# A decoder block's mixer: products of the chunk kernel over four column groups, the first convolution tap on ScalarE, low parts of weights split at other places

## What is computed

```
x = x + 1/2 * SwiGLU(RMSNorm(x))
h = RMSNorm(x); [u | v | gates] = h @ w_in          # 1024 -> 5120
y_a = GLU(GELU(S5(u)))          # 64 groups of 16 channels, 64 complex states each, + d_skip * u
y_b = ConformerConv(v)          # z = val * sigmoid(gate); causal depthwise conv of 31 taps; LayerNorm, SiLU, pointwise
x = x + (sigmoid(g_A) * y_a + sigmoid(g_B) * y_b) @ w_out
x = x + 1/2 * SwiGLU(RMSNorm(x)); final RMSNorm
```

## Time and profile before

| | us |
|---|---|
| median of 3 runs (lowest, highest) | 2216.61 (2214.64, 2218.44) |
| the profiled execution's own time | 2219.29 |
| its span, first to last instruction | 2217.5 |
| TensorE busy in the span | 2166.0 (98%) |
| VectorE busy | 1683.7 (76%) |
| ScalarE busy | 949.2 (43%) |
| GpSimd busy | 632.4 (29%) |

### The profile page before, as it was taken

The page is one execution under the profiler, slowest core; times in us unless marked ns, Lnnn a source line. Parts: engine busy times, 40 slices in busy tenths (PEclk is TensorE's granted clock), DMA queues, the critical chain, the costliest instruction groups (busy, mean ns, idle before and its releaser), DMA issues.

```text
span 2217.5 us, 31528 instructions
## 1 busy us (share of the span) xinstructions
PE 2166.0 (98%) x10238; PEld 1787.2 (81%) x10238; DVE 1683.7 (76%) x2123; ACT 949.2 (43%) x1551; POOL 632.4 (29%) x714
## 2 busy tenths in 40 slices
PE   7999999999999999999999999999999999999998
PEld 6788788787878888888887788878878888888886
DVE  5877777868996999999998649454597777665557
ACT  5455455544455122222223224135355555554444
POOL 2886645969980000000000430000014442000000
PEclk9999999999999999999999999999999999999999
DMA  5234876478774344544535632553247665337764
GB/s 169 77 118 149 260 231 220 147 258 295 261 262 148 100 143 145 148 135 147 148 112 166 199 105 81 194 189 124 72 141 229 208 215 164 109 118 253 233 193 171
DMA packets 306625, 379.07 MB, mean 171 GB/s; under 512 B 27257, under 2 KB 199377, under 8 KB 306416
## 3 DMA queue, kind: packets, MB, share of 16 engines
q1 hardware_dynamic: 286576, 306.01, 43.5%
q0 software_dynamic: 18800, 67.85, 9.2%
q10 hardware_dynamic: 1168, 4.20, 0.5%
HBM read 256.06 MB, written 119.55 MB: 169 GB/s over the span
## 4 chain that ended last, share of the span: by engine, by line
PE 82%; DVE 10%; ACT 3%; DMA 3%; issue 2%; SPq 1%; DVEq 0%; ACTq 0%
PE PU L1396 10%; PE PU L1398 10%; PE PU L1397 10%; PE PU L1336 9%; PE PU L1338 9%; PE PU L1337 9%; PE PD L1271 3%; PE PD L1273 3%; PE PD L1272 3%; PE PU L1271 2%; PE PU L1272 2%; PE PU L1273 2%; DVE Alo L2074 2%; PE PD L1472 1%; DVE Dlo L2071 1%
## 5 line engine op out<-in xcount | busy, mean ns | idle before, releaser
L1336 PE MATMUL PU<-Hhi,Whi 128*128 128x512 f32 x896 | 352.5, 393 | 3.3 <-DVE Hlo L2508 2.5
L1338 PE MATMUL PU<-Hhi,Wlo 128*128 128x512 f32 x896 | 348.8, 389 | 0.0
L1337 PE MATMUL PU<-Hlo,Whi 128*128 128x512 f32 x896 | 348.8, 389 | 0.0
L2487 DVE SCALAR_TENSOR_TENSOR XT<-XT,wq 128x1024 f32<-128x1024 f32 x240 | 313.3, 1305 | 8.2
L1336 PEld LDWEIGHTS PU<-Hhi,Whi 128*128 128x128 f32 x896 | 168.2, 188 | 42.3 <-DVE Hlo L2508 3.9
L1338 PEld LDWEIGHTS PU<-Hhi,Wlo 128*128 128x128 f32 x896 | 168.2, 188 | 35.0
L1337 PEld LDWEIGHTS PU<-Hlo,Whi 128*128 128x128 f32 x896 | 168.3, 188 | 34.9 <-issue 0.7
L1396 PE MATMUL PU<-Hhi,Dhi 128*128 128x512 f32 x480 | 187.0, 389 | 2.0 <-ACT s1b L1748 2.0
L1397 PE MATMUL PU<-Hlo,Dhi 128*128 128x512 f32 x480 | 186.7, 389 | 0.0
L1398 PE MATMUL PU<-Hhi,Dlo 128*128 128x512 f32 x480 | 186.7, 389 | 0.0
L1271 PE MATMUL PD<-Dhi,Ahi 128*128 128x512 f32 x352 | 138.0, 392 | 3.5 <-DVE Alo L2074 3.4
(11 more groups left out here) (400 smaller groups left out, 5166.3 us busy)
## 6 DMA issues: line engine op xcount, KB each, us to landing
TAB<-in_w_ffn_down POOLq DMA_DIRECT2D x44, 512.0 KB, 5.0
d_sb<-TAB POOLq DMA_DIRECT2D x44, 512.0 KB, 4.0
Wraw<-in_w_ffn_up SPq DMA_DIRECT2D x80, 256.0 KB, 3.8
XT<-in_w_ffn_up SPq DMA_DIRECT2D x80, 256.0 KB, 4.4
d_sa<-XT SPq DMA_DIRECT2D x80, 256.0 KB, 2.4
Wraw<-in_w_in SPq DMA_DIRECT2D x32, 512.0 KB, 5.1
d_act<-G SPq DMA_DIRECT2D x48, 256.0 KB, 2.8
WRd<-d_sb SPq DMA_DIRECT2D x44, 256.0 KB, 4.1
```

Source lines behind the costliest of these rows:

```text
L1336: mm(o_, Whi[s][:, side, k, :], Hhi[:, k, hs[h]], start=k == 0, stop=False)
L1337: mm(o_, Whi[s][:, side, k, :], Hlo[:, k, hs[h]], start=False, stop=False)
L1338: last = mm(o_, Wlo[s][:, side, k, :], Hhi[:, k, hs[h]], start=False, stop=k == KT - 1)
L2487: stt(CVb, z_, w_, CVb, ALU.mult, ALU.add).then_inc(m["conv"], 1)
```

## The change

Five things change together.

1. `kernel_of_chunk`: pair pr writes to output partitions 32\*pr to 32\*pr + 15 of the bank, the loop over a is the outer one. The number of matmuls, their rows, columns and moving lengths stay.
2. K then lies as KK[pr\*32 + i, g2, 128]. ACT copies it with 112x128 per bank. Four DMAs store it to a new DRAM scratch d_k in the old layout, SP waits until they have landed, and the 8 loads of MT read from d_k. d_skip (dvec, dq, dd) gets the matching layout, with three more small GpSimd operations (eye4) and one more transpose and copy at the start.
3. Tap 0 is made by ACT, `scale * Z + bias`, into a buffer CV0 of its own (the unused second half of Dlo), right after z_rep and before the copy of y; DVE's tap 1 reads CV0 and writes CV.
4. The low part of the gates' pair (q, 1) is made by DVE at the start of step q, after the products z, no longer at the end of step q - 1. The low part of pair (q+1, 0) comes after taps 1 to 8. On ACT the high part of pair (q+1, 0) moves behind the first half of UE.
5. SP's `conv_store(q - 1)` moves ahead of the loads for pair (q+1, 0).

```diff
@@ scratch, tiles
+    d_k = scratch("d_k", [SG, GQ, P])
+    CV0 = over("Dlo", 4 * D, "CV0", [P, L])[:, :]
-    KK = KKf.rearrange("p (g n) -> p g n", g=GQ)
+    KROWS = (PR - 1) * 32 + SG
+    KK = KKf[0:KROWS, 0:2 * P].rearrange("p (t n) -> p t n", t=2)
-    TAP_STOPS = 0, 13, 16, 17, 23, TAPS
+    K_D = 1 + 16 * PR
+    TAP_STOPS = 1, 9, 13, 16, 17, TAPS
@@ SP, mix_loads
+            if not first:
+                conv_store(q - 1)
             if last:
                 glu_pair(0, R_GLU)
             else:
                 mix_pair(q + 1, 0)
                 mix_unit(q + 1)
             if not first:
-                conv_store(q - 1)
                 sp.wait_ge(m["chain"], q * ROT)
...
-            sp.wait_ge(m["k_d"], q + 1)
+            sp.wait_ge(m["k_d"], q * K_D + 1)
+            for pr in range(PR):
+                sp.dma_start(d_k[:, 2 * pr:2 * pr + 2, :], KK[pr * 32:pr * 32 + SG]).then_inc(m["k_d"], 16)
+            sp.wait_ge(m["k_d"], q * K_D + K_D)
             for jr in range(J):
                 j = J - 1 - jr
-                sp.dma_start(MT[jr * SG:(jr + 1) * SG, :, j * SG:P], KK[0:SG, :, 0:(jr + 1) * SG])\
-                  .then_inc(m["mt_ld"], 16)
+                sp.dma_start(MT[jr * SG:(jr + 1) * SG, :, j * SG:P], d_k[:, :, 0:(jr + 1) * SG])                  .then_inc(m["mt_ld"], 16)
@@ PE, kernel_of_chunk
-            for pr in range(PR):
-                for a in range(2):
+            for a in range(2):
+                for pr in range(PR):
                     for g2 in range(2):
-                        last = mm(PD[g2][0:SG, pr * P:(pr + 1) * P], BA[half[g2], a, pr, 0:SG],
-                                  CA[half[g2], a, pr, 0:J * SG], start=a == 0, stop=a == 1)
+                        last = mm(PD[g2][pr * 32:pr * 32 + SG, 0:P], BA[half[g2], a, pr, 0:SG],
+                                  CA[half[g2], a, pr, 0:J * SG], start=a == 0, stop=a == 1, skip_group_check=True)
@@ ACT, kernel_of_chunk and mix
-                fn(KK[0:SG].rearrange("i (r a) n -> i a r n", a=2)[:, g2],
-                   PD[g2][0:SG, :].rearrange("i (r n) -> i r n", n=P), ACT.Copy).then_inc(m["k_sb"], 1)
+                fn(KK[:, g2], PD[g2][0:KROWS, 0:P], ACT.Copy).then_inc(m["k_sb"], 1)
...
-            split_pair(r + 2, 0)
-            if not first:
-                act.wait_ge(m["y_full"], q)
-                evacuate_y()
...
             fn(Z[:, 0:J - 1, PAD:PAD + C], Z[:, J:ZB, PAD - 1:PAD - 1 + C], ACT.Copy).then_inc(m["z_rep"], 1)
+            act.wait_ge(m["wq"], q * 3 + 3)
+            fn(CV0.rearrange("p (b c) -> p b c", b=J), Z[:, J - 1:ZB, PAD:PAD + C], ACT.Identity, bias=wq[:, TAPS:TAPS + 1],
+               scale=wq[:, TAPS - 1:TAPS]).then_inc(m["conv"], 1)
+            if not first:
+                act.wait_ge(m["y_full"], q)
+                evacuate_y()
             for h in range(2):
                 act.wait_ge(m[f"u_full{h}"], q + 1)
                 wait(act, m["u_saved"], q * 16)
                 fn(UE[:, hs[h]], PD[h][:, :], ACT.Copy).then_inc(m["u_sb"], 1)
+                if h == 0:
+                    split_pair(r + 2, 0)
@@ DVE, taps and mix
-                if s == 0:
+                dve.wait_ge(m["conv"], q * TAPS + s)
+                if s == 1:
                     dve.wait_ge(m["z_rep"], q + 1)
-                    dve.wait_ge(m["wq"], q * 3 + 3)
                     wait(dve, m["cv_saved"], q * 16)
-                    ts(CVb, z_, w_, wq[:, TAPS:TAPS + 1], ALU.mult, ALU.add).then_inc(m["conv"], 1)
-                else:
-                    dve.wait_ge(m["conv"], q * TAPS + s)
-                    stt(CVb, z_, w_, CVb, ALU.mult, ALU.add).then_inc(m["conv"], 1)
+                stt(CVb, z_, w_, (CV0 if s == 1 else CV).rearrange("p (b c) -> p b c", b=J), ALU.mult, ALU.add)\
+                    .then_inc(m["conv"], 1)
...
-            split_pair(r + 2, 0)
+            if not first:
+                split_pair(r + 1, 1)
             stops = TAP_STOPS
             taps(q, stops[0], stops[1])
+            split_pair(r + 2, 0)
+            taps(q, stops[1], stops[2])
             if not first:
                 gelu_in(q - 1)
-            taps(q, stops[1], stops[2])
+            taps(q, stops[2], stops[3])
             if not first:
                 gelu_out(q - 1)
             if not last:
                 split_unit(q + 1, 0)
-            taps(q, stops[2], stops[3])
+            taps(q, stops[3], stops[4])
...
             if not last:
-                taps(q, stops[3], stops[4])
-                split_pair(r + 3, 1)
                 taps(q, stops[4], stops[5])
```

More of the change, by code:

```diff
@@ L239, in build @@
     wdw = sb("wdw", [P, KT, TAPS])
-    dvec = sb("dvec", [SG, NG])
+    dvec = sb("dvec", [P, 2, KT])
     wq = sb("wq", [P, TAPS + 1])
-    dq = sb("dq", [SG, GQ])
+    dq = sb("dq", [P, 2])
     xf = XT[:, :, :].rearrange("p k n -> p (k n)")
@@ L260, in build @@
     prow = tf[0:NP, 0:3 * P].rearrange("r (a n) -> r a n", a=3)
-    rows = tf[0:NG, 3 * P:4 * P + SG]
-    ldt = tf[0:NP, 4 * P + SG:4 * P + SG + 2]
+    rows = tf[0:NG, 3 * P:5 * P]
+    ldt = tf[0:NP, 5 * P:5 * P + 2]
     Bb = rt.rearrange("p (a r i) -> p a r i", a=2, i=SG)
@@ L275, in build @@
     Bsc = sb("Bsc", [P, PR * C // 2])
-    dd = sb("dd", [SG, GQ, SG])
+    dd = sb("dd", [P, 2, SG])
+    eye4 = sb("eye4", [P, SG])
     BA = TAB[:, T_BAR:T_CAR].rearrange("p (a r n) -> p a r n", a=2, n=J * SG)
@@ L830, in _ @@
                         pattern=[[-1, P]], channel_multiplier=1).then_inc(const, 1)
+        pool.wait_ge(const, 3)
+        g.tensor_tensor(eye4[:, :], ident[:, 0:SG], ident[:, 32:32 + SG], ALU.add).then_inc(const, 1)
+        for c in (2, 3):
+            pool.wait_ge(const, c + 2)
+            g.tensor_tensor(eye4[:, :], eye4[:, :], ident[:, 32 * c:32 * c + SG], ALU.add).then_inc(const, 1)
         n = 0
@@ L842, in _ @@
                  (ldt[:, :], ssm_log_dt[0].rearrange("(r a) -> r a", a=2)),
-                 (rows[0:NG, P:P + SG], ssm_d[0].rearrange("(g i) -> g i", i=SG))]
+                 (rows[0:KT, P:2 * P], ssm_d[0].rearrange("(k p) -> k p", p=P))]
         vec = [norm_mix_g[0], norm_ffn2_g[0], norm_final_g, conv_dw_b[0], conv_ln_g[0], conv_ln_b[0]]
@@ L1172, in mix @@
             wait(pool, m["dd"], q)
-            g.tensor_copy(dq[:, :], dvec[:, bass.ds(q * GQ, GQ)]).then_inc(m["wq"], 1)
+            g.tensor_copy(dq[0:KROWS, :], dvec[0:KROWS, :, bass.ds(q, 1)].rearrange("p t a -> p (t a)")).then_inc(m["wq"], 1)
             pool.wait_ge(m["wq"], q * 3 + 3)
-            wait(pool, m["k_d"], q)
-            g.tensor_tensor(dd[:, :, :], ident[0:SG, 0:SG].unsqueeze(1).to_broadcast([SG, GQ, SG]),
-                            dq[:, :].unsqueeze(2).to_broadcast([SG, GQ, SG]), ALU.mult).then_inc(m["dd"], 1)
+            wait(pool, m["k_d"], q * K_D)
+            g.tensor_tensor(dd[0:KROWS], eye4[0:KROWS, :].unsqueeze(1).to_broadcast([KROWS, 2, SG]),
+                            dq[0:KROWS, :].unsqueeze(2).to_broadcast([KROWS, 2, SG]), ALU.mult).then_inc(m["dd"], 1)
             pool.wait_ge(m["dd"], q + 1)
             pool.wait_ge(m["k_sb"], q * 2 + 2)
-            g.tensor_tensor(KK[0:SG, :, 0:SG], KK[0:SG, :, 0:SG], dd[:, :, :], ALU.add).then_inc(m["k_d"], 1)
+            g.tensor_tensor(KK[:, :, 0:SG], KK[:, :, 0:SG], dd[0:KROWS], ALU.add).then_inc(m["k_d"], 1)
+        pool.wait_ge(const, 6)
         mix(0)
@@ L1237, in params @@
             tr(PD[0][:, 96:96 + 7 * KT], rows[0:7 * KT, 0:P], ident[0:7 * KT, 0:7 * KT]).then_inc(row_tr, 1)
-            tr(PD[0][0:SG, 160:160 + NG], rows[0:NG, P:P + SG], ident[0:NG, 0:NG]).then_inc(row_tr, 1)
+            tr(PD[0][:, 160:160 + KT], rows[0:KT, P:2 * P], ident[0:KT, 0:KT])
+            tr(PD[0][0:KROWS, 168:168 + KT], rows[0:KT, P + SG:2 * P], ident[0:KT, 0:KT]).then_inc(row_tr, 1)
             pe.wait_ge(dw_ld, 16)
@@ L1661, in params @@
             fn(vecs[:, KT:7 * KT], PD[0][:, 96 + KT:96 + 7 * KT], ACT.Copy).then_inc(vec_in, 1)
-            fn(dvec[:, :], PD[0][0:SG, 160:160 + NG], ACT.Copy).then_inc(vec_in, 1)
+            fn(dvec[:, 0], PD[0][:, 160:160 + KT], ACT.Copy)
+            fn(dvec[0:KROWS, 1], PD[0][0:KROWS, 168:168 + KT], ACT.Copy).then_inc(vec_in, 1)
             fn(wdw[:, :, :].rearrange("p k t -> p (k t)"), PD[0][:, 256:256 + KT * TAPS], ACT.Copy).then_inc(dw_in, 1)
```

## The result

| | before | after |
|---|---|---|
| median of 4 runs, us | 2217.04 (2214.64 to 2218.44) | 2255.57 (2253.12 to 2258.70) |
| ratio, 95% interval | | 1.0176 (1.0161 to 1.0191) |
| span of the profiled execution | 2217.5 | 2254.6 |

The kernel became 38.5 us slower. The forecast was 2237; the measured time lies at the very end of the range of 2206 to 2256, twice as far from the kernel before as was said (38.5 us, not 20.4).

The account below looks back on a forecast made before the run. PE (TensorE), busy 63.32 us, was taken to bound each step. Net of K's saving, +0.6 (step 0), +14.4 (steps 1 to 6), +2.4 (step 7) and one clock fall of 3.0 gave +20.4: 2237 us, range 2206 to 2256.

Parts of the forecast that it names:

- The clock: PE after its wait for UG: clock granted at one half for 6.8 us, costing 3.0 us, taken to strike once.
- The waits: PE before delta, waiting for UG: 1.9 us in step 0, 3.7 us in each later step.
- K: Matmuls of kernel_of_chunk over four column groups: 1.86 us falls to 0.55, 1.3 off PE per step, 10.4 in all.
- Tap 0 on ACT: DVE loses 0.85 us and a 1.22 us wait; ACT gains a pass of 1.06 to 1.16; DVE does not wait.
- The low parts and SP's queue: Low part of (q+1, 0) after 8 taps delays SP's pair loads by 7.5 us, then u's store and UG; PE waits 3.7.
- e: Zero point of a step's times: ACT begins the second gate sigmoid, PE having just ended the step's conv pair.
- Step 0: First mixer step, without y_load: u's store lands at 23.5, UG at 29.0, PE waits 1.9 us, net +0.6.
- rival C: Clock falls at every wait: seven times 3.0 us on top of 17.4, 2255 us; chance 0.20.
- MT through DRAM: K's stores and MT's loads by way of DRAM end at e + 41, PE needs MT at 65.7: no cost.
- conv_store: Going first on SP it costs nothing, as the pair behind it waits for the low part of (q, 1) anyway.
- Rival A: Store of u overtakes or pair loads pass quickly: PE never waits, 10.4 us gained, 2206 us; chance 0.21.
- Rival B: Column groups bring nothing, K stays at 1.86 us and UG is in time: 2216 us, no change; chance 0.12.

Follow-up runs that it names:

- e3: The kernel before with only K over four column groups and MT by way of DRAM: 2207.5 us, against 2217.6 beside it.
- e6: The kernel before with only tap 0 moved to ScalarE, into CV0: 2218.4 us, ratio 0.9999 to 1.0018.
- e1: The changed kernel with SP's loads for pair (q+1, 1) put behind the 8 loads of UG: 2211.4 us.
- e5: The changed kernel with 6 taps in place of 8 ahead of the low part of pair (q+1, 0): 2230.9 us.
- e2: The changed kernel with K made as before (one column group, no d_k): 2256.1 us against 2255.6.
- e4: The changed kernel with 7 taps in place of 8 ahead of the low part of pair (q+1, 0): 2244.5 us.

## Why the prediction was right and wrong

**Where the 18 us went.** The forecast added 20.4 us, the change cost 38.5. The clock was put at 3.0 and took 11.4, 8.4 more. The waits were put at 27.8 (1.9 + 7 x 3.7) and took 36.5, 8.7 more, 4.1 of it in step 0. K was put at 10.4 saved and saved 9.6, 0.8 less. That makes 17.9 of the 18.1.

**K.** Right: 1.3 us a step was said, 1.20 measured, and e3 shows 10.1 us for the kernel where 10.4 were said. The four rounds of eight in the last section are what the sum assumed, eight places side by side with four of the 32 each; the trace does not name the places. The column places and the order of the loops changed together, and no run takes them apart.

**Tap 0 on ACT.** Right: nothing, by e6. DVE did wait 0.20 us for CV0, which took 1.23 us against the 1.06 to 1.16 said.

**The low parts and SP's queue.** Right in mechanism, each link a little late: pair loads at e + 16.4 (16.6 measured), YC at 23.5 (24.4, from 863.68 + 6.4 - 845.68), u's store landed at 25.3 (25.7), the wait 3.7 (4.3), DVE's wait for GELU 3.5 (4.5). Steps 1 to 6 waited 4.5 us in the mean, not 3.7, some 5 us for the kernel. The y stores were put at e + 6 to 10 and called harmless; they went out from e + 8.4 to 12.5, and in e1 it is their landing that sends u's store out at e + 16.7, where 15.5 was expected.

**Step 0.** Wrong: "wait 1.9, net +0.6" was put down, 6.0 was measured. UG's time was right: its eight loads went out from 735.45 on, so with the 5.5 it landed at about 740.95, e + 28.8 (e is 712.17), where 29.0 was said. What failed is when PE wants it: I used the 28.4 of a full step, but step 0 has no `s5_outputs` (1.95 and 2.06 us on lines 1454 and 1458 in step 2), so PE was done with K at 735.39 = e + 23.2. That is 4 us. PE's timeline there:

```profile
734.73 0.66 PE L1471 MATMUL PD<-TAB 64*16 64x128 f32 x32
741.35 3.31 PE L1507 MATMUL PD<-XT,RT 128*64 128x128 f32 x32 [5.96 <-DMA XT<-d_u]
```

**The clock.** The step that failed: "I take it to strike once: +20.4". In the profiled execution it struck at all eight waits, and delta grew by 11.4 us where 3.0 stood. The record I had the earlier trace rows had a fall after a wait shorter than the one I forecast, so by the forecast's own numbers the fall each time, rival C, was the likelier reading; it was discounted as a single case. (e5's 3.12 us without a fall shows that one case was thin indeed; at the 3.4 to 6.0 us of this kernel none was spared.) The price was missed the other way: 3.0 us a fall was said, 1.4 measured (11.4 / 8), because seven of the eight falls lasted some 3.4 us instead of the 6.8 of rows 11, and the longer one, in step 0, lay in good part in the wait, with PE busy for only 2.75 us of it:

```profile
737.30:744.10 6.80, 2.75 (x26) 2.76 (x28) 2.65 (x3) 0.00 (x0) 0.37 (x1) 0.50 0.56 150
```

Eight falls of 1.4 make the 11.4. C's 2255 met the time with seven falls at 3.0 and waits that were 9 us too short: two errors of opposite sign.

**MT through DRAM, conv_store, the start.** MT and the start: right, nothing, by e3. conv_store's early place had no run of its own. In step 2 of the changed kernel SP's wait ahead of its pair loads is for DVE's low parts, as forecast (`SPq L460 <- DVE Wlo L2079: 8.5, 2, 4.6`), so it is not conv_store that held them there. In one step of the changed kernel SP issued MT's loads at 880.04 to 885.1, 28 us before the step's end.

**Rival A** (the u store overtakes) fell with the 6.7 us of that store and the eight waits. **Rival B** (column groups bring nothing) fell with K's 0.66 us; its warning, that a late UG hides K's gain, is what e2 shows.

## What to carry to other kernels

Before moving a step that frees a buffer, read the queue behind the load that waits for this buffer. Here a 2 us subtraction, delayed by eight taps, held up the store and the loads of u that TensorE needed, and put 1.5 MB in front of them. Issue first what the bound engine waits for, and prefetches for the next step behind it; and when a wait of several microseconds on TensorE is forecast, price its half clock at every occurrence, even if the trace has only one earlier record of it. Of several edits made together, run each alone: here K was worth 10 us, tap 0 nothing that could be measured, the order a loss of 40 us, and the sum hid the first.

## What the runs showed of the hardware that was not expected

All 32 matmul records of K in step 2 of the changed kernel began within 0.41 us, the first eight of them within 0.06 (line 1471 alone, busy times of PE and weight loads with the number of instructions, clock, DMA share, GB/s):

```profile
872.22:872.27 0.06, 0.05 (x8) 0.05 (x14) 1.00 0.00 0
...
872.20:872.34 0.14, 0.12 (x8) 0.12 (x16) 1.00 0.04 15
872.20:872.45 0.25, 0.23 (x16) 0.23 (x24) 1.00 0.14 43
872.20:872.55 0.35, 0.33 (x24) 0.33 (x32) 1.00 0.28 86
872.20:872.61 0.41, 0.39 (x32) 0.37 (x32) 1.00 0.36 111
```

They come in four rounds of eight, 0.10 to 0.13 us apart. Over all that is one record each 13 ns. The kernel's 16 float32 matmuls stand as two records each; counted as 16 they come one each 26 ns in the mean, but the first eight records, four matmuls if the two records of one stand together, begin within 0.06 us, under 20 ns from one to the next. The floor of about 25 ns from start to start that the prediction quoted from the Trainium skill (TensorE: Matmul & The Clock Gate, "Wait — 56ns, not 53.3ns?") is therefore not seen within a round, for small matmuls on different places of the array, and all 32 took 0.66 us, not the 0.8 estimated by it; the measurement decides.

A granted clock of one half came with waits of PE in stretches of about 3.4 or 6.8 us, which began within the wait or up to 1.2 us into the work behind it. Which of the two lengths it was differed between steps of one kernel after nearly the same wait (e4: 3.17 and 3.27 us), and for waits of 2.4 to 3.1 us so did whether it came at all. What decides it stays open.
